# Attention scores as products of 64 rows: two heads on the two row halves of the array, q and k as plain hi and lo tiles

## The reference, cut to what matters

```python
h = rms_norm(x, norm_mix[i])
proj = (h @ w_in[i]).astype(f32)
qa, ka, va, qb, fb, ib, gb, qc, kc, vc = jnp.split(proj, split_at, axis=-1)
...
s = jnp.einsum('brnqhe,brnkhe->brnhqk', qs, kk) * (E ** -0.5) + bias
s = jnp.where(valid[:, None], s, NEG_BIG)
m = lax.stop_gradient(jnp.max(s, axis=-1, keepdims=True))
pexp = jnp.exp(s - m)
den = jnp.sum(pexp, axis=-1, keepdims=True)
o = jnp.einsum('brnhqk,brnkhe->brnqhe', pexp / den, vv)
...
x = x + mix @ w_out[i]
x = x + (jax.nn.silu(ug) * uv) @ w_down[i]
```

## Time and profile before

| what | us |
|---|---|
| runs: median (lowest to highest of 3) | 724.6 (723.93 to 724.86) |
| profiled execution: span from first to last instruction | 723.0 |
| TensorE busy (matmuls) | 713.9 (99%) |
| DVE, ACT, POOL busy | 444.1, 314.1, 132.6 |
| products of the scores, L714 and L716 | 147.3 to 254.2 us of the span, 48 of each |

### The profile page before, as it was taken

How to read it: one execution, slowest core, us unless ns; L and a number is a source line. 1 busy time by engine, 2 the same in 40 slices (tenths; PEclk the granted TensorE clock), 3 DMA queues, 4 the chain that set the end, 5 groups by cost and what they waited for, 6 DMA issues and landing times.

```text
span 723.0 us, 10532 instructions
## 1 busy us (share of the span) xinstructions
PE 713.9 (99%) x3931; PEld 590.1 (82%) x3931; DVE 444.1 (61%) x722; ACT 314.1 (43%) x512; POOL 132.6 (18%) x104
## 2 busy tenths in 40 slices
PE   9999999999999999999999999999999999999995
PEld 7778888888888888888888888888888888888885
DVE  4775678497766736577667667667663243334536
ACT  5792223366566634543334334334332222125834
POOL 1015232045565412110110110110110000000000
PEclk9999999999999999999999999999999999999999
DMA  8433222322222113243332332332316323333202
GB/s 272 122 97 105 60 66 77 121 58 90 87 88 89 58 31 116 87 117 88 99 105 87 94 109 87 91 111 87 93 45 189 110 80 110 97 92 115 90 0 117
DMA packets 117425, 69.44 MB, mean 96 GB/s; under 512 B 2818, under 2 KB 112466, under 8 KB 117386
## 3 DMA queue, kind: packets, MB, share of 16 engines
q1 hardware_dynamic: 115374, 65.39, 30.5%
q10 hardware_dynamic: 2012, 3.52, 1.5%
HBM read 66.77 MB, written 2.13 MB: 95 GB/s over the span
## 4 chain that ended last, share of the span: by engine, by line
PE 98%; DVE 1%; issue 0%; ACT 0%; DVEq 0%; ACTq 0%
PE bank L584 27%; PE bank L586 26%; PE bank L585 26%; PE bank L956 2%; PE bank L954 2%; PE bank L955 2%; PE bank L629 2%; PE bank L745 2%; PE bank L728 2%; PE bank L714 1%; PE bank L716 1%; PE bank L799 1%; PE bank L788 1%; PE bank L700 0%; PE bank L966 0%; PE bank L672 0%
## 5 line engine op out<-in xcount | busy, mean ns | idle before, releaser
L584 PE MATMUL bank<-h_hi,w_hi 128*128 128x512 f32 x582 | 230.6, 396 | 0.0
L586 PE MATMUL bank<-h_hi,w_lo 128*128 128x512 f32 x582 | 227.1, 390 | 0.0
L585 PE MATMUL bank<-h_lo,w_hi 128*128 128x512 f32 x582 | 226.8, 390 | 0.0
L1026 ACT ACTIVATE w_hi<-raw 128x1024 fp32r<-128x1024 f32 (+1 forms) x104 | 108.0, 1040 | 259.5 <-PE bank L586 251.2
L1416 DVE TENSOR_TENSOR w_lo<-raw,w_hi 128x1024 fp32r<-128x1024 f32 (+1 forms) x104 | 127.7, 1228 | 90.1 <-ACT w_hi L1026 89.9
L586 PEld LDWEIGHTS bank<-h_hi,w_lo 128*128 128x128 f32 x582 | 109.2, 188 | 23.4
L584 PEld LDWEIGHTS bank<-h_hi,w_hi 128*128 128x128 f32 x582 | 109.3, 188 | 22.6 <-issue 1.1
L585 PEld LDWEIGHTS bank<-h_lo,w_hi 128*128 128x128 f32 x582 | 109.4, 188 | 21.0 <-issue 0.2
L1972 POOL TENSOR_SCALAR probs<-probs,row_inv 128x512 f32<-128x512 f32 (+3 forms) x48 | 62.5, 1308 | 72.1 <-DVE row_inv L1649 71.9
L584 PE MATMUL bank<-act_hi,w_hi 128*128 128x512 f32 x176 | 68.6, 389 | 0.0
L586 PE MATMUL bank<-act_hi,w_lo 128*128 128x512 f32 x176 | 68.5, 389 | 0.0
(11 more groups left out here) (259 smaller groups left out, 959.7 us busy)
## 6 DMA issues: line engine op xcount, KB each, us to landing
raw<-in_w_up SPq DMA_DIRECT2D x44, 512.0 KB, 3.6
raw<-in_w_in SPq DMA_DIRECT2D x26, 512.0 KB, 3.7
raw<-in_w_down SPq DMA_DIRECT2D x16, 512.0 KB, 3.4
raw<-in_w_out SPq DMA_DIRECT2D x8, 512.0 KB, 3.4
raw<-in_w_pg SPq DMA_DIRECT2D x8, 512.0 KB, 3.8
bias<-bias_table ACTq DMA_DIRECT2D x6, 512.0 KB, 3.7
raw<-in_w_down SPq DMA_DIRECT2D x8, 384.0 KB, 3.1
x_rows<-in_x SPq DMA_DIRECT2D x4, 512.0 KB, 5.2
```

Source lines behind the costliest of these rows:

```text
L584: pe.matmul(bank, hi, x_hi, start=first, stop=False)
L585: pe.matmul(bank, hi, x_lo, start=False, stop=False)
L586: return pe.matmul(bank, lo, x_hi, start=False, stop=last)
L1026: act.activation(w_hi[:, u % SPLIT, 0:nk * ncol], raw[:, u % RAW, 0:nk * ncol], ACT.Copy)\
```

## The change

Each of q and k becomes two plain tiles of 128 rows, hi and lo, in which the first head of a pair has rows 0 to 63 and the second rows 64 to 127. A head's scores are three products of 64 rows: q_hi·k_hi, q_lo·k_hi and q_hi·k_lo. `step_scores` issues them at even ticks only, for both heads of the pair, in turn: first head, second head, for each of the three. The even step's head writes bank score[0], the odd one's score[1]. TensorE waits for `logits` n at even n. Odd ticks keep their transposes and have no scores. `split_piece` does one copy on ACT and one difference on DVE for each q and each k; the zeros of k_lo and their semaphore are gone, as is the wait for it. Borrowed uses of these tiles (weights of the fourth unit, the parts of a sum, the first warming products) are moved to the new names with the same sizes. A padding tile keeps the addresses behind them.

```diff
@@ -305,9 +305,8 @@
 
-        q_both = sb("q_both", [P, 3, 2, SEQ], F32R, mixing)
-        k_both = sb("k_both", [P, 3, 2, SEQ], F32R, mixing)
-        k_lo = sb("k_lo", [P, 3, 2, SEQ], F32R, mixing)
+        q_hi, q_lo, k_hi, k_lo = (sb(n, [P, 3, SEQ], F32R, mixing) for n in ("q_hi", "q_lo", "k_hi", "k_lo"))
+        sb("after_keys", [P, 6, SEQ], F32, mixing)
         v_tok = sb("v_tok", [P, 3, TT, P], F32, mixing)
@@ -455,7 +454,7 @@
         fourth = [v_tok[:, 0:2, :, :].rearrange("p a t c -> p (a t c)")]
-        fourth += [k_both[:, n, :, :].rearrange("p a n -> p (a n)") for n in range(2)]
+        fourth += [t[:, 0:2, :].rearrange("p a n -> p (a n)") for t in (k_hi, k_lo)]
 
@@ -700,21 +699,24 @@
 
-            def step_score(n):
-                head, i = head_of(n), tile_of(n)
-                pair = head // 2
-                if n % (2 * TT) < 2:
-                    pe.wait_ge(q_ready, 2 * pair + head % 2 + 1)
-                    pe.wait_ge(k_ready, 4 * pair + 2 * (head % 2) + 2)
+            def step_scores(n):
+
+                pair, keys, queries = head_of(n) // 2, (tile_of(n) + 1) * P, slice(tile_of(n) * P, (tile_of(n) + 1) * P)
+                if n % (2 * TT) == 0:
+                    pe.wait_ge(q_ready, pair + 1)
+                    pe.wait_ge(k_ready, pair + 1)
                 if n >= 2:
-                    pe.wait_ge(logits, n - 1)
-                if n == 0:
-                    pe.wait_ge(k_lo_blank, 2)
-                keys, hh, queries = (i + 1) * P, head % 2, slice(i * P, (i + 1) * P)
-                pe.matmul(score[n % 2][:, 0:keys], q_both[:, pair % 3, hh, queries], k_both[:, pair % 3, hh, 0:keys],
-                          start=True, stop=False)
-                pe.matmul(score[n % 2][:, 0:keys], q_both[:, pair % 3, hh, queries], k_lo[:, pair % 3, hh, 0:keys],
-                          start=False, stop=True).then_inc(scored, 1)
+                    pe.wait_ge(logits, n)
+                heads = [slice(hh * HEAD, (hh + 1) * HEAD) for hh in range(2)]
+                for hh in range(2):
+                    pe.matmul(score[hh][:, 0:keys], q_hi[heads[hh], pair % 3, queries], k_hi[heads[hh], pair % 3, 0:keys],
+                              start=True, stop=False)
+                for hh in range(2):
+                    pe.matmul(score[hh][:, 0:keys], q_lo[heads[hh], pair % 3, queries], k_hi[heads[hh], pair % 3, 0:keys],
+                              start=False, stop=False)
+                for hh in range(2):
+                    pe.matmul(score[hh][:, 0:keys], q_hi[heads[hh], pair % 3, queries], k_lo[heads[hh], pair % 3, 0:keys],
+                              start=False, stop=True).then_inc(scored, 1)
 
@@ -752,8 +754,8 @@
                     values_of_pair((m - VALUE_LAG) // (2 * TT))
-                if m < STEPS:
-                    step_score(m)
+                if m < STEPS and m % 2 == 0:
+                    step_scores(m)
 
@@ -1104,17 +1106,15 @@
                 kind, i, _ = GROUPS[GROUP_OF[slot - 1]]
-                if kind not in ("q", "k") or n >= 2:
+                if kind not in ("q", "k") or n:
                     return
-                if n == 0:
-                    wait_taken(act, GROUP_OF[slot - 1])
-                    if i >= 3:
-                        act.wait_ge(scored, 2 * TT * (i - 2))
-                own = slice(n * HEAD, (n + 1) * HEAD)
+                wait_taken(act, GROUP_OF[slot - 1])
+                if i >= 3:
+                    act.wait_ge(scored, 2 * TT * (i - 2))
                 if kind == "q":
-                    act.activation(q_both[own, i % 3, n, :], scratch[own, 0, :], ACT.Copy).then_inc(q_hi_ready, 1)
+                    act.activation(q_hi[:, i % 3, :], scratch[:, 0, :], ACT.Copy).then_inc(q_hi_ready, 1)
                 else:
-                    act.activation(k_both[own, i % 3, n, :], scratch[own, 1, :], ACT.Copy).then_inc(k_hi_ready, 1)
+                    act.activation(k_hi[:, i % 3, :], scratch[:, 1, :], ACT.Copy).then_inc(k_hi_ready, 1)
 
@@ -1407,7 +1407,7 @@
         def _(dve):
-            dve.memset(q_both[:, 0, 0, :].bitcast(F32), 0.0).then_inc(blank_ready, 1)
+            dve.memset(q_hi[:, 0, :].bitcast(F32), 0.0).then_inc(blank_ready, 1)
 
@@ -1497,7 +1497,7 @@
                     if i:
-                        dve.wait_ge(q_ready, 2 * i)
+                        dve.wait_ge(q_ready, i)
                     queries, r_back = (bass.AP(tensor=t.tensor, offset=t.offset + P - 1, ap=[[SEQ, P], [P, TT], [-1, P]])
@@ -1505,7 +1505,7 @@
 
-                        dve.wait_ge(k_ready, 4 * i)
+                        dve.wait_ge(k_ready, i)
                     times_r(scratch[:, 1, :], bank[:, :]).then_inc(acc_taken, 1)
@@ -1548,16 +1548,14 @@
                 kind, i, _ = GROUPS[GROUP_OF[slot - 1]]
-                own, other = (slice(h * HEAD, (h + 1) * HEAD) for h in (hh, 1 - hh))
-                if kind == "q" and 0 <= hh < 2:
-                    dve.wait_ge(q_hi_ready, 2 * i + hh + 1)
-                    dve.tensor_tensor(q_both[other, i % 3, hh, :], scratch[own, 0, :],
-                                      q_both[own, i % 3, hh, :].bitcast(F32), ALU.subtract).then_inc(q_ready, 1)
-                elif kind == "k" and 0 <= hh < 2:
-                    dve.wait_ge(k_hi_ready, 2 * i + hh + 1)
-                    dve.tensor_copy(k_both[other, i % 3, hh, :], k_both[own, i % 3, hh, :].bitcast(F32)).then_inc(k_ready, 1)
-                    dve.tensor_tensor(k_lo[own, i % 3, hh, :], scratch[own, 1, :], k_both[own, i % 3, hh, :].bitcast(F32),
-                                      ALU.subtract).then_inc(k_ready, 1)
+                if kind == "q" and hh == 0:
+                    dve.wait_ge(q_hi_ready, i + 1)
+                    dve.tensor_tensor(q_lo[:, i % 3, :], scratch[:, 0, :], q_hi[:, i % 3, :].bitcast(F32), ALU.subtract)\
+                       .then_inc(q_ready, 1)
+                elif kind == "k" and hh == 0:
+                    dve.wait_ge(k_hi_ready, i + 1)
+                    dve.tensor_tensor(k_lo[:, i % 3, :], scratch[:, 1, :], k_hi[:, i % 3, :].bitcast(F32), ALU.subtract)\
+                       .then_inc(k_ready, 1)
 
@@ -1929,13 +1927,6 @@
             pool.wait_ge(filled, 1)
-            for hh in range(2):
-                other = slice((1 - hh) * HEAD, (2 - hh) * HEAD)
-                if hh:
-                    pool.wait_ge(k_lo_blank, hh)
-                pool.memset(k_lo[other, :, hh, :].bitcast(F32), 0.0).then_inc(k_lo_blank, 1)
-            pool.wait_ge(k_lo_blank, 2)
-
             pool.memset(first_ones[:, :].bitcast(F32), 1.0).then_inc(ones_set, 1)
```

More of the change, by code:

```diff
@@ L375, in build @@
         tok_mean = stat[:, 3, 0:1]
-        sum_parts, sum_ones = k_lo[:, 0, :, :], k_lo[:, 1, 0, 0:P]
+        sum_parts, sum_ones = k_lo[:, 0:2, :], k_lo[:, 2, 0:P]
         p_rows = conv_g[:, 0:2, :].rearrange("p a n -> p (a n)").rearrange("p (t c) -> p t c", t=TT)
@@ L413, in build @@
         z_chain, kin_arg, log_f, g_ready, kin_ready = (sem(s) for s in ("z_chain", "kin_arg", "log_f", "g_ready", "kin_ready"))
-        f_ready, tot_ready, corner_zero, k_lo_blank = (sem(s) for s in ("f_ready", "tot_ready", "corner_zero", "k_lo_blank"))
+        f_ready, tot_ready, corner_zero = (sem(s) for s in ("f_ready", "tot_ready", "corner_zero"))
         gate_ready, bq_ready = sem("gate_ready"), sem("bq_ready")
@@ L787, in keep_warm @@
                 for _ in range(count):
-                    pe.matmul(banks[2][:, :], q_both[:, 0, 0, 0:P], q_both[:, 0, 0, :], start=True, stop=True)
+                    pe.matmul(banks[2][:, :], q_hi[:, 0, 0:P], q_hi[:, 0, :], start=True, stop=True)
             def turn_x(j):
```

## The result

| what | before | after |
|---|---|---|
| runs on one chip: median (lowest to highest of 5), us | 724.75 (723.93 to 724.87) | 729.94 (729.55 to 730.32) |
| profiled execution: span, us | 723.0 | 727.8 |
| TensorE busy, us | 713.9 | 717.4 |
| DVE, ACT, POOL busy, us | 444.1, 314.1, 132.6 | 429.1, 305.4, 129.0 |

What follows compares the result with a forecast made beforehand. TensorE, busy 713.9 of 723.0 us, was taken to bound the kernel. Products and mode +4.5 and waits +1.3 made +5.8, a span of 728.8; with 1.6 for the median, 730.4 us, range 727.2 to 737.

Steps and rivals of the forecast that it cites:

- A pair costs one product: Score products on TensorE: two products on row halves take the time of one, 3.8 us less in all.
- rival 3: Score pairs: the two halves' products run one after the other, another 11.3 us, 741.8 us; chance 0.08.
- rivals 1 and 2: Score pairs: halves overlap only in part, 734.2 us, chance 0.10; the halves' weight loads take turns, 736.4, chance 0.12.
- A visit costs 0.40: Double steps: passing from whole array to row halves and back costs 0.40 us a visit, 8.6 us more in all.
- the 0.05 for the longer first load: First score weight load of a visit: 128 columns, 191 ns against 137, lies bare, 0.05 us more a visit.
- the emptying: Array at a mode change: part of the 0.15 us read at the values; 0.09 passes under each wait.
- Rival 4: Mode change at the scores: hardware passes between halves and whole without emptying, crossing not paid, 722.1 us; chance 0.07.
- rival 5: Double steps: a visit at 0.13 to 0.2 us and few waits, 723.2 to 726 us; chance 0.05.
- A crossing alone behind the values: Five double steps right behind values, where the array already changes mode: one added crossing, 0.20 us each.
- the return at 128 keys: Third product at 128 keys: no next load before the crossing, 0.06 us instead of 0.11, 0.3 less over six.
- The waits, 1.3: TensorE at steps 2, 22, 46 waits for the odd step's row minimum: 0.4 + 0.7 + 0.5 - 0.3 = 1.3 us more.
- Costs at nothing: POOL's two start memsets, ACT's merged half copies and the borrowed unit at the start: no effect on the time.

Runs made afterwards that it cites:

- e_whole3: The changed kernel with each pair of 64-row products made one product of 128 rows into the first head's bank, no change of mode: 723.58 us.
- e_lone64: The kernel before, with only the second product of each step on the head's own 64 rows, 48 visits of one product: 741.95 us.
- e_18_visits: e_minima with the scores of 128 keys computed in the visit of those of 384, 18 visits in place of 24: 727.32 us.
- e_minima: The changed kernel with both row minima of a double step in a row on DVE at the even step: 729.2 us.
- e_double: The kernel before, its 128-row products kept, but both heads' scores at the even step with one wait for `logits`: 727.56 us.
- e_in_turn: The changed kernel with a double step's three products of the first head issued first, then the three of the second: 730.39 us.

## Why the prediction was right

**A pair costs one product** (3.8 us less): held. Pairs follow at 0.23, 0.17, 0.12 and 0.11 us, their products 3 ns apart; that refutes rival 3 (0.23 apart within a pair) and rivals 1 and 2 (a third more; never nearer than 0.22). The weight loads of the two halves do not take turns: they start 3 to 4 ns apart. They are no longer than those of 128 rows, 185 ns against 191 in the earlier trace rows (group by line, mean ns):

```profile
L718 PEld LDWEIGHTS bank<-k_lo,q_hi 64*128 64x128 f32 x48 | 4.5, 185 | 0.3
```

The column halves of the values were a true guide to the row halves: 0.109 us a pair there, 0.11 at 128 keys here.

**A visit costs 0.40** (8.6 us more): held, four ways. 0.39 to 0.40 by distances in the changed kernel, 0.38 by e_whole3, 0.365 by e_lone64, 0.35 by e_18_visits. Each experiment changes a little more than the visit, so I take 0.35 to 0.40; the two lowest figures hold visits of 128 keys, where part of the price comes back. With the 0.05 for the longer first load the terms gave the price that was measured, but no run varied that load, so the 0.05 remains my estimate. Nor does any run show the emptying that the prediction counts in its 0.15 and, as 0.09, takes off each wait: what the runs showed in its place is 0.20 us more by distance at each end of a visit, 0.09 and 0.10 of it ahead of the first start there. Rival 4 (the crossing is not paid) and rival 5 (paid at less than 0.2) fall with this. A crossing alone behind the values cost 0.19 (0.20 forecast), the return at 128 keys 0.05 as forecast. Products and mode together: 4.3 measured, 4.5 forecast.

**The waits, 1.3**: held in place and, more luckily, in size. They are at steps 2, 22 and 46 and nowhere else; by distance 0.37, 0.58 and 0.37, where the three terms less a third of the 0.3 each gave 0.3, 0.6 and 0.4. e_minima shows that they are DVE's order: the two that it could reach went. Their size was right because TensorE came nearly as late as I had assumed, late by the very visits; e_whole3, where it came earlier, shows that they would have been 2.7 had the visits cost nothing. Rival 4's 722.1 was thus too low in itself: e_whole3 has its terms but for the 0.3 at 128 keys, and took 723.6.

**Costs at nothing**: held. The wait at the start is 1.5 us as before, the projections and the rest are within 0.02 us, and the 27 us taken from the other engines move nothing but the new waits. e_double adds what I had put in one sentence only: the relief of DVE keeps 1.3 us of waits out of the changed order, at steps 4 and 40.

**The sum**: 5.8 forecast, 5.6 in the stage, 5.2 in the medians. What I had not foreseen is the start, which made the first profiled pair differ by 4.8; by spans alone the terms would have looked a fifth too large.

**What was wrong** were three expectations: that the waits of e_whole3 would stay as they were, that a pair has to be issued side by side, and, by 1.4 us, the price of the 48 visits of e_lone64 (743.3 expected, 741.95 measured).

**Why it could not pay.** A double step saves one product of four, 0.11 to 0.23 us, and pays a visit of 0.35 to 0.40. All products saved and the 0.3 at 128 keys are 4.1 us; at 0.39 a visit they pay, by estimate, for some 10 visits, and the changed order has 24 (18 in e_18_visits).

## What to carry to other kernels

Before splitting a product over halves of the array, count how often the array goes from whole to split and back, and set that against the products saved; each stay cost 0.35 to 0.40 us here, with one product in it or with twelve, so gather what shares a mode. When one engine's wait is for two results in place of one, the other engine's order must bring the two together as well, or it hands the time back, 0.94 us here. And measure a small change by the distances between starts in its own stage, where the repeats here agreed to 0.04 us, not by two spans.

## What the runs showed of the hardware

- Products of different row halves passed each other in the queue: the second half's product started 10 ns after the first half's, though two products stood between them (e_in_turn).
- A lone product of 64 rows was dearer than the same one over 128 rows with zeros: 0.365 us more (e_lone64). In the changed kernel, at a visit of 512 keys, the price by distance is 0.09 us ahead of the visit's first product and 0.10 ahead of the first full product behind it, and 0.10 to 0.11 more behind each of these two, whose weight loads start only with them. The distances are measured; what takes the time in each of them was not tested.
- Weight loads of 64 rows and 128 columns took 183 to 186 ns, against 191 for 128 rows, and those of the two halves start 3 to 4 ns apart: both loaded in the time of one.
